# The convolution stage of a gated-linear-attention mixer, moved from 64 plain weight units to eight passes of eleven products with tokens on partitions

## The reference, cut to what matters

```python
(q, k, v, g_out, gk_low, gate_b, gate_c, xc, merge_a, merge_b) = split(h @ w_in)
o   = rmsnorm(gla_chunked(q, k, v, log_g), gla_norm_w)      # four heads, value width 512 each
y_a = o * silu(g_out)
u   = gate_c * xc
y_b = gate_b * (w[0] * u[t-2] + w[1] * u[t-1] + w[2] * u[t])   # causal, per channel
merged = sigmoid(merge_a) * y_a + sigmoid(merge_b) * y_b
out = merged @ w_out
```

## Time and profile before

| | |
|---|---|
| median of 3 runs | 2605.47 us (2604.85 to 2606.33) |
| profiled execution, its own time | 2606.42 us |
| its span, first to last instruction | 2604.6 us |
| TensorE busy | 2590.4 us, 99% |
| VectorE busy | 2083.6 us, 80% |
| ScalarE busy | 1402.2 us, 54% |
| mean DMA rate | 191 GB/s |

### The profile page before, as it was taken

How to read it: one execution, slowest core, us unless ns; L and a number is a source line. 1 busy time by engine, 2 the same in 40 slices (tenths; PEclk the granted TensorE clock), 3 DMA queues, 4 the chain that set the end, 5 groups by cost and what they waited for, 6 DMA issues and landing times.

```text
span 2604.6 us, 34491 instructions
## 1 busy us (share of the span) xinstructions
PE 2590.4 (99%) x13138; PEld 2208.1 (85%) x13138; DVE 2083.6 (80%) x1902; ACT 1402.2 (54%) x1331; POOL 3.5 (0%) x8
## 2 busy tenths in 40 slices
PE   9999999999999999999999999999999999999998
PEld 8888888888888888888888888888888888888887
DVE  7886666679967999879998878897777787677888
ACT  6554444456756565546565556536554455444454
POOL 0000000000000000000000000000000000000000
PEclk9999999999999999999999999999999999999999
DMA  6464454546564646555655554534455545555554
GB/s 246 175 226 176 178 184 176 184 170 222 180 243 176 226 177 225 184 207 179 225 182 210 190 218 162 176 143 178 162 181 190 184 170 210 206 183 191 187 220 142
DMA packets 71892, 497.52 MB, mean 191 GB/s; under 512 B 8183, under 2 KB 9432, under 8 KB 12648
## 3 DMA queue, kind: packets, MB, share of 16 engines
q1 hardware_dynamic: 71784, 496.06, 52.6%
HBM read 493.93 MB, written 2.10 MB: 190 GB/s over the span
## 4 chain that ended last, share of the span: by engine, by line
PE 95%; DVE 2%; ACT 1%; DMA 1%; issue 0%; SPq 0%; DVEq 0%; ACTq 0%
PE acc L2540 27%; PE acc L2598 20%; PE acc L2548 14%; PE acc L2605 10%; PE acc L2623 6%; PE acc L2617 5%; PE acc L2619 5%; PE acc L2734 1%; DVE w_lo L1459 1%; ACT w_hi L852 1%; PE acc L2958 1%; DMA mask_s<-in_mask 1%; PE acc L2742 1%; PE aux L3040 1%; PE aux L3099 1%; DMA raw<-in_w_down 0%
## 5 line engine op out<-in xcount | busy, mean ns | idle before, releaser
L852 ACT ACTIVATE w_hi<-raw 128x2048 fp32r<-128x2048 f32 (+1 forms) x483 | 921.3, 1909 | 723.3 <-PE acc L2540 265.7
L1459 DVE TENSOR_TENSOR w_lo<-raw,w_hi 128x2048 fp32r<-128x2048 f32 (+1 forms) x483 | 1099.8, 2280 | 188.9 <-ACT w_hi L852 178.2
L2540 PE MATMUL acc<-xa,w_hi 128*128 128x512 f32 x3104 | 743.0, 391 | 0.0
L2540 PEld LDWEIGHTS acc<-xa,w_hi 128*128 128x128 f32 x3104 | 571.4, 188 | 112.3 <-issue 0.7
L2548 PEld LDWEIGHTS acc<-xa,w_lo 128*128 128x128 f32 x3104 | 397.9, 191 | 15.0
L2548 PE MATMUL acc<-xa,w_lo 128*128 128x256 f32 x3104 | 402.9, 283 | 0.0
L2598 PE MATMUL acc<-w_hi,xa 128*128 128x512 f32 x1152 | 273.2, 389 | 0.0
L2598 PEld LDWEIGHTS acc<-w_hi,xa 128*128 128x128 f32 x1152 | 215.9, 188 | 44.8
L2598 PE MATMUL acc<-w_hi,hid 128*128 128x512 f32 x768 | 183.3, 390 | 1.4 <-ACT w_hi L852 1.4
L1471 DVE TENSOR_TENSOR tmp<-acc,small 128x512 f32<-128x512 f32 x76 | 52.5, 691 | 150.7 <-ACT small L862 150.4
L2598 PEld LDWEIGHTS acc<-w_hi,hid 128*128 128x128 f32 x768 | 143.5, 188 | 32.0 <-ACT w_hi L852 2.2
(11 more groups left out here) (423 smaller groups left out, 2954.5 us busy)
## 6 DMA issues: line engine op xcount, KB each, us to landing
raw<-in_w_in SPq DMA_DIRECT2D x158, 1024.0 KB, 4.8
raw<-in_w_gate_up SPq DMA_DIRECT2D x88, 1024.0 KB, 4.8
raw<-in_w_down SPq DMA_DIRECT2D x88, 1024.0 KB, 4.8
raw<-in_w_up SPq DMA_DIRECT2D x87, 1024.0 KB, 4.8
raw<-in_w_out SPq DMA_DIRECT2D x32, 1024.0 KB, 4.8
raw<-in_w_uq SPq DMA_DIRECT2D x3, 1024.0 KB, 4.9
h_tok<-in_x_tok SPq DMA_DIRECT2D x1, 2048.0 KB, 10.7
raw<-in_w_ukv SPq DMA_DIRECT2D x4, 512.0 KB, 3.2
```

What stands on the lines that cost most here:

```text
L852: act.activation(hi_part(u, run)[:, 0:kt * P], raw_of(u)[:, 0:kt * P], ACT.Copy).then_inc(hi_made, splits(u, run))
L1459: dve.tensor_tensor(lo_part(u, run)[:, 0:kt * P], raw_of(u)[:, 0:kt * P], hi_part(u, run)[:, 0:kt * P], ALU.subtract).then_inc(lo_made, sp ...
L2540: last = pe.matmul(acc[:, bnk], w_hi[:, u % SPLIT, k * P:(k + 1) * P], x[:, k0 + k], start=first and k == 0, stop=False)
```

## The change

The four projections of the convolution stage become eight passes (`CONV_STARTS`), two per head: an even pass makes `gate_c` and `xc`, an odd (second) pass `merge_b` and `gate_b`. The product of each pair is formed with tokens on partitions in `halves` (`conv_product`), transposed by TensorE into `aux` (`turn_product`), and from there ACT takes the middle tap (`middle_taps`) and DVE the outer two (`outer_taps`) and the gate product (`gated_conv_out`). Scores and value products of a head stand in its even pass; `stage` of the next head stands in its odd pass, behind form GM_2. The last transposition falls into the first output-gate pass. In the second block weight sum 1 and the splits of M_1 move into the last gated pair, and two ACT copies change place with a split. Core of the diff, by engine:

```diff
 # layout, units
-U_CONV, N_CONV = U_V + 2 * GATE_FORMS, 64
+U_CONV, N_CONV = U_V + 2 * GATE_FORMS, 2 * HEADS * GATE_FORMS
+CONV_STARTS = tuple(U_CONV + GATE_FORMS * _k for _k in range(2 * HEADS))
 # SP
-            load(U_CONV, d["w_in"][32:], N_CONV, 2048)
-            for hd, u in enumerate(OUT_STARTS):
-                gate_loads(u, d["w_in"][32 + N_CONV + 8 * hd:], hd == 0)
+            for n, u in enumerate(CONV_STARTS + OUT_STARTS):
+                gate_loads(u, d["w_in"][32 + 8 * n:], False)
 # ACT (the loop of 16 units per head with head_part is gone)
+            def conv_gate(hd):
+                for c in range(2):
+                    act.wait_ge(acc_free, T_CONV + 8 * hd + 4 + c + 5)
+                    act.activation(halves[:, c], halves[:, c], ACT.Sigmoid, scale=rstd_t[:, c:c + 1]).then_inc(gate_out, 2)
+            for k, u in enumerate(CONV_STARTS):
+                hd, second = k // 2, k % 2
+                for form in range(GATE_FORMS):
+                    if form == GM_7:
+                        conv_state(k, GM_7, 3, 1)
+                    split(u + form + 2)
+                    if form == GM_1 and not second:
+                        value_high(hd)
+                    if form == GM_5:
+                        if k:
+                            act.wait_ge(turned, k + 1)
+                        conv_state(k, GM_1, 3, 0)
+                    if form == GATE_2:
+                        conv_state(k, GM_5, 2, 3)
+                    if form == GM_6:
+                        conv_state(k, GM_6, 3, 2)
+                        if second:
+                            middle_taps(hd)
+                        else:
+                            act.wait_ge(masked, hd + 1)
+                            act.activation(sc_hi[:], sc[:], ACT.Copy).then_inc(sc_hi_made, 1)
+                    if form == GM_2:
+                        prepare(ACT.Sigmoid if second else ACT.Sqrt)
+                    if form == GM_7 and not second:
+                        act.wait_ge(o_made, hd + 1)
...
+                    if form == UP_1 and not second:
+                        act.wait_ge(var_made, hd + 2)
+                        act.activation(o_var[:], o_var[:], ACT.Sqrt).then_inc(std_made, 1)
+                    if form == GM_4 and not second:
+                        act.wait_ge(o_scale, hd + 1)
+                        for c in range(2):
+                            act.activation(v_tok[:, hd, c], aux[:, c], ACT.Copy, scale=o_rstd[:, c:c + 1]).then_inc(o_read, 1)
+                if second:
+                    conv_gate(hd)
 # DVE
+            def conv_product(k):
+                conv_sum(k, UP_2, 2, 2, 3)
+                conv_sum(k, UP_2, 3, 3, 2)
+                dve.wait_ge(acc_free, T_CONV + 4 * k + 8)
+                if k % 2:
+                    dve.wait_ge(gate_out, 2 * k + 4)
+                for c in range(2):
+                    dve.scalar_tensor_tensor(halves[:, c], halves[:, 2 + c], (rstd_t if k % 2 else rstd_2)[:, c:c + 1], halves[:, c],
+                                             ALU.mult, ALU.mult).then_inc(gate_in, 1)
+            for k, u in enumerate(CONV_STARTS):
+                hd, second = k // 2, k % 2
+                if k:
+                    conv_product(k - 1)
+                for form in range(GATE_FORMS):
+                    split(u + form + 2)
+                    if form == GATE_1:
+                        weight_sum(u, 2)
+                    if form == GM_5:
+                        weight_sum(u, 3)
+                        if not second:
+                            value_low(hd)
+                    if form == GATE_2 and not second:
+                        dve.wait_ge(scores_made, hd + 1)
+                        dve.tensor_tensor(sc[:], aux[:, 0, 0:3 * P], mask_s[:], ALU.mult).then_inc(masked, 1)
+                    if form == GM_3:
+                        weight_sum(u, 4)
+                        if not second:
+                            dve.wait_ge(sc_hi_made, hd + 1)
+                            dve.tensor_tensor(sc_lo[:], sc[:], sc_hi[:], ALU.subtract).then_inc(o_parts_made, 1)
+                    if form == GM_7:
+                        if second:
+                            outer_taps(hd)
+                        elif hd:
+                            gated_conv_out(hd - 1)
+                    if form == GM_2 and second and hd + 1 < HEADS:
+                        stage(hd + 1)
+                    if form == UP_1:
+                        conv_sum(k, GM_2, 0, 0, 1)
+                        conv_sum(k, GM_4, 1, 1, 4)
+                        if not second:
+                            dve.wait_ge(o_squared, 2 * hd + 2)
+                            dve.tensor_scalar(o_var[:], o_sum[:], 1.0 / DV, EPS, ALU.mult, ALU.add).then_inc(var_made, 1)
+                    if form == GM_4:
+                        if not second:
+                            dve.wait_ge(std_made, hd + 2)
+                            dve.reciprocal(o_rstd[:], o_var[:]).then_inc(o_scale, 1)
+                        weight_sum(u + GATE_FORMS, 1)
+            conv_product(2 * HEADS - 1)
 # PE
                 by_tokens(u + GATE_1, b_11, xa, 8, 4, True, False)
+                if scores:
+                    scores()
                 pe.wait_ge(acc_free, b_22 + 1)
                 product(u + GM_1, b_22, *block_of(xa, 0, 0), first=True, final=True)
                 if turn:
                     turn()
...
                 product(u + GM_2, b_11, *block_of(xa, 4, 0), final=True)
+                if values:
+                    values()
+            def scores(hd):
+                pe.wait_ge(staged, hd + 1)
+                pe.wait_ge(gate_in, 4 * hd + 2)
...
+            def head_values(hd):
+                pe.wait_ge(o_parts_made, 3 * hd + 3)
...
+            def turn_product(k):
+                pe.wait_ge(gate_in, 2 * k + 4)
+                pe.wait_ge(*((op_f32, 4 * (k // 2)) if k % 2 else (o_read, k + 2)))
...
 # second block, ACT and DVE
-                        if not (last and p) and not (ahead == 2 and p == 0):
+                        if not (ahead == 2 and p == 0):
                             split(u + 4, run)
+                        if last and p:
+                            weight_sum(u0 + 2 * GT, 1)
+                            split(u0 + 2 * GT + M_1)
-                gated(2 * GT - 4, GT - 2)
-                weight_sum(u0 + 2 * GT, 1)
+                gated(2 * GT - 4, GT - 2, last=True)
```

More of the change, by code:

```diff
@@ L952, in _ @@
                         value_state(u, GM_6, t + 3, 2 * p + 1, 0)
[L953 to L983, removed]
+            act.sem_inc(small_made, T_OUT - T_V)
@@ new lines, in conv_state, with value_high, middle_taps @@
+            def conv_state(k, form, tile, n):
+                act.wait_ge(lo_used, CONV_STARTS[k] + form + 1)
+                act.activation(halves[:, n], acc[:, bank(T_CONV + 4 * k + tile)], ACT.Copy).then_inc(snapped, 1)
+            def value_high(hd):
+                act.wait_ge(acc_free, T_V + 4 * (hd // 2) + 8)
+                act.activation(v_hi[:], v_tok[:, hd], ACT.Copy).then_inc(o_parts_made, 1)
+            def middle_taps(hd):
+                for t in range(4):
+                    i = 4 * hd + t
+                    act.activation(yb[:, i], aux[:, t // 2, t % 2 * S:(t % 2 + 1) * S], ACT.Copy,
+                                   scale=column("conv_w", i + 2 * DT)).then_inc(conv_mid, 1)
@@ new lines, in value_low, with outer_taps @@
+            def value_low(hd):
+                dve.wait_ge(o_parts_made, 3 * hd + 1)
+                dve.tensor_tensor(v_lo[:, hd], v_tok[:, hd], v_hi[:], ALU.subtract).then_inc(o_parts_made, 1)
+            def outer_taps(hd):
+                for back in (1, 2):
+                    for t in range(4):
+                        i = 4 * hd + t
+                        if back == 1:
+                            dve.wait_ge(conv_mid, i + 1)
+                        elif t == 0:
+                            step.wait()
+                        tail = yb[:, i, back:S]
+                        step(dve.scalar_tensor_tensor(tail, aux[:, t // 2, t % 2 * S:(t % 2 + 1) * S - back],
+                                                      column("conv_w", i + (2 - back) * DT), tail, ALU.mult, ALU.add))
@@ L1781, in _ @@
                         weight_sum(u, 4)
-                    if form == GM_7 and hd:
-                        merged(hd - 1)
+                    if form == GM_7:
+                        if hd:
+                            merged(hd - 1)
+                        else:
+                            gated_conv_out(HEADS - 1)
                     if form == UP_1:
@@ L2391, in _, with gated @@
                 v0, g0 = V_FF2 + g * GT, G_FF2 + g * GT
-                def gated(run, pairs, ahead=0, between=None):
+                def gated(run, pairs, ahead=0, between=None, last=False):
                     for p in range(2):
@@ new lines, in head_values @@
+            def head_values(hd):
```

(6 more changed lines are left out.)

176 lines of the change are left out of this document (64 added, 112 removed).

## The result

| | before | after |
|---|---|---|
| median | 2605.9 us (2604.85 to 2606.44, 4 runs) | 2632.6 us (2630.87 to 2633.13, 4 runs) |
| profiled execution | 2606.42 us | 2632.17 us |
| its span | 2604.6 us | 2630.3 us |

The account below looks back on a forecast made before the run. TensorE's instruction stream was taken to bound the kernel, with DVE's order adding waits. -22.9 + 14.4 + 15.6 + 6.8 + 1.0 - 1.9 = +13.0 us gave a median of 2618.5 us, range 2607 to 2628.

Parts of the forecast that it names:

- The stream, -22.9: Convolution stage: TensorE's own work falls from 373.44 to 350.5 us, 22.9 us less if it never waits.
- (a): Value product of each head: `sc_lo` stands behind GM_7's split and weight sum 4; TensorE waits 3.6 us four times, 14.4 us.
- (b): Second pass of heads 0 to 2, up to the next scores: DVE has no gap; 5.2 us wait three times, 15.6 us.
- (c): End of each first pass: the variance root's round trip through ACT delays GM_1's bank; four waits, 6.8 us in all.
- staging's share: Second passes of heads 0 to 2: staging, free before, costs 3.07 us each, 9.2 us of (b).
- (d): First output-gate pass: the same wait as (b) without staging and products, 1.0 us, bounds 0 and 2.
- The second block, -1.9: Start of the down projection: the earlier split of M_1 brings a load forward; all TensorE's 1.9 us of waits won.
- The clock, 0: Granted clock stays 1.00 in the stage; term 0, since the trace showed no full waits in mid-kernel.
- the rival: Clock falls in the stage's waits, one to four times: +4 to +14 us, middle 2626 us; chance 0.15.
- DVE keeps up: DVE makes up (b) and (c) elsewhere: 2595 us with only (a) left, chance 0.06; without (a) 2580.7 us, 0.05.
- Staging hidden: Second passes: 3 us of lead in the splits behind staging makes (b) 6.4 us, time 2609.3 us; chance 0.10.

Follow-up runs that it names:

- filled kernel: Against the kernel after: 14 unread matmuls ahead of each value product and 13 ahead of the scores of heads 1 to 3; 2622.64 us, ratio 1.0066.
- last experiments: Kernel with all moves, `sc_lo` back behind weight sum 4: 2611.13 us; the same with 14 unread matmuls ahead of each value product: 2601.93 us.
- filled kernels: The filled kernel, 2622.64 us, and the same with staging in the first pass and 11 unread matmuls ahead of the scores, 2612.9 us.
- kernel with all moves: Against the kernel after: `sc_lo` earlier, staging in first pass, root and scaled copies later on ACT, scores of heads 1 to 3 behind the transposition; 2586.55 us.
- the one with the value waits filled: Kernel with all moves, but `sc_lo` back behind weight sum 4 and 14 unread matmuls ahead of each value product; 2601.93 us, ratio 0.9986.
- the one with the value waits alone: Kernel with all moves, but `sc_lo` back behind weight sum 4; 2611.13 us, ratio 1.0017.

## Why the prediction was right in sign and wrong in size

From the stage's start to the end of the first output-gate pass TensorE's own stream is 350.5 + 40.8 = 391.3 us. The filled kernel takes 432.47, so waits cost 41.2 us (forecast 37.8). The kernel after takes 442.09: 9.6 us for the clock (forecast 0). What is behind it took 1999.6 us before and 1997.4 after: -2.2 (forecast -1.9). The forecast 13.0 + 3.4 + 9.6 - 0.3 = 25.7 us is the difference of the two spans.

**The stream, -22.9, held.** With nearly all waits gone the nine passes take 397.25 us, 17.0 less than before, 6.0 over the 391.3 of the sum. Of these 3.2 are the four waits of GM_1 shown for that kernel, which cost a little more than their idle time. Its first pass, 45.12 us, is the 40.82 + 4.21 of the sum to 0.1.

**(a), 14.4 us, held nearly:** 15.4 by the medians of the last experiments, 14.9 by their passes. The forecast 3.6 each was a reading of idle time (3.4 in the list); a pass grew by 48.85 - 45.12 = 3.7 us, since the matmuls next to the wait take longer steps too (221.13 to 221.47 in the timeline above, where 0.23 is usual).

**(b), 15.6 us, was the term with the largest error of the waits.** In the filled kernel the passes of head 0 are 45.94 - 41.71 = 4.2 over a second pass without waits, 1.5 of it (c), and the next first pass is 52.99 - 45.92 (40.82 + 0.89 + 4.21) - 3.8 of (a) = 3.3 over: 6.0 per head, 18.0 us. With DVE's 27.8 and a lead of 268.29 - 267.88 = 0.41 us (TensorE's start of GM_7 in the row below, DVE's above) the forecast's own sum gives 27.8 - 0.4 - 21.8 = 5.6. The step that failed is that it took one wait for all of it: the list shows it in pieces (L2684, L2666 and L2937), and, as in (a), each piece costs a little over its idle time.

```profile
268.29 0.39 PE L2678 MATMUL acc<-w_hi,v_hi 128*128 128x512 f32 x1
```

Of (b), staging's share, **9.2 us, was right**: 9.0 by passes in the filled kernels and 9.5 from the kernel with all moves.

**(c), 6.8 us, held.** The list has 6.5 for this line, of which 0.8 is (d), so 5.7 us of idle time in four waits, and each costs a few tenths more; moving two lines on ACT took these four away. **(d), 1.0 us, held**: 42.79 - 41.71 = 1.1.

**The second block, -1.9, was right in sum and wrong in cause.** The stretch behind the stage is 2.2 us shorter, but "I take all of TensorE's 1.9 us as won" by the edits fails: undoing them costs 0.56 us at most and 0.14 in this stretch. The other 2.0 us stayed with them undone; that the load of the earlier trace rows landed earlier fits it, but neither this nor its cause was tested.

**The clock, 0, is the step that failed, with 9.6 us.** The prediction said that an idle stretch about as long as the wait in (a) is followed by the lower clock, gave the rival a chance of 0.15 and 4 to 14 us, and then took "by the trace of full waits in mid-kernel (none) the term is 0". That no such wait was in the trace of before was no evidence that it would be harmless: the change itself brought seven of about 3 us. Of the two reasons against the rival, that the waits of (b) are cut into pieces fell too: the scores' own idle time is 2.97 us, and it was followed by the lower clock all three times. The rule of the Trainium skill cited there ("TensorE: Matmul & The Clock Gate", section "What's actually happening") is the one the trace agrees with, as far as it goes: granted clock 0.50 behind waits of 2.97 and 3.43 us, in five of seven cases. The rival's price was right and its chance too low. With 9.6 us in the sum the forecast would have been near 2628; what is still missing to 2632.6 is mostly the 3.4 us by which the waits were over their forecast, 2.4 of them in (b).

**The rivals.** "DVE keeps up" needed waits under 24.8 us; they were 41.2, although DVE was only 82% busy. "Staging hidden" fell by 9.0 and 9.5 us. That the right order makes the change a gain is shown by the kernel with all moves: -22.9 us of stream and only 6.0 given back.

## What to carry to other kernels

Where splits are issued just two forms ahead, ask of every small operation what stands before it in its engine's queue when its reader comes, not how busy that engine is: at the same 2168 us of DVE work (and with two moves on DVE, one on ACT and one on TensorE) two orders were 46 us apart. Where a change brings TensorE waits of some 2 to 3.5 us into a dense stream, price the lower clock behind each (here 9.6 us for five falls, 10.6 for four longer ones), and measure a term that is in dispute from a version without the other waits, or with them filled by unread matmuls; otherwise the clock takes back part of what a repair gives, as it did with 5.6 of 9.0 us here.

## What the hardware showed beyond the forecast

- In the profiled execution of the kernel after, the granted clock was 0.50 after five of its seven long waits (value product of heads 0 and 1, scores of heads 1 to 3), and 1.00 after the value products of heads 2 and 3, which waited just as long (the value products start at 425.55 and 527.85 us):

```profile
425.00:429.00 4.00, 3.45 (x15) 2.88 (x16) 2.69 (x3) 0.00 (x0) 0.00 (x0) 1.00 0.61 213
527.50:531.50 4.00, 3.65 (x16) 3.04 (x17) 2.50 (x2) 0.00 (x0) 0.00 (x0) 1.00 0.65 227
```

  With staging in the first pass it fell after all seven, though the three waits for scores were shorter (2.4 us at most). So whether one wait is followed by a fall was not to be read from its length alone; what decides it stays open.
- Kernels with such waits scatter. Of the six whose clock stayed at 0.999 four repeat within 0.25 to 1.24 us, the filled one within 2.1 and the one with the value waits filled within 4.1 (one run of ten stands apart); the one with staging and `sc_lo` moved ranges over 8.3 us, the one with the value waits alone over 5.3.
- Unread matmuls cost nothing in place of a wait: 95 of them made the kernel 10.0 us faster, 56 of them 9.2.
